# Every second quad's last 704 words of the last down unit as a transfer of its own, from an input laid out for it

## The chip, the cores and the metric

The kernel runs on one core of one Trainium2 chip. What is measured is the time on the device in microseconds (us) of one execution of the whole program; times of several runs are given as their median. The profile shows one execution.

## The reference, cut to what matters

The program is a decoder trunk of two layers for 256 tokens of width 1024 in float32. Each layer has a token mixer (heads of stick-breaking attention and retention in layer 0, sliding-window attention in layer 1) and then a mixture of experts, on which this change works:

```python
def expert_block(args):
    xb, e = args
    h = jax.nn.silu(xb @ w_gate[e]) * (xb @ w_up[e])
    return h @ w_down[e]
```

There are 32 experts in each layer, with `w_gate` and `w_up` of 1024 x 512 and `w_down` of 512 x 1024 floats: 6 MB an expert, 192 MB a layer. Each token goes to two of them. Every expert's weights are read once per layer.

## The kernel before

**Tiling.** The 32 experts of a layer are taken as 8 quads of four experts. A quad's weights are 12 units: 4 of gate, 4 of up and 4 of down. A unit is 128 partitions by `UNIT` = 4096 words (2 MB), and partition p of a unit is one contiguous run in HBM. The weights rest in SBUF in slots of one unit each. Eight of them (`LOOP_SLOTS`) form a ring for the loop over the quads.

**Loading.** SyncE (`sp`) issues all loads of weights, one queue, in a fixed order. Within `experts(l)`, quads 0 and 1 are loaded unit by unit. After that a loop runs `half` times (here 3): `quad(2 * t, 1)` and `quad(2 * t + 1, 0)`. A quad of the first sort is loaded by three transfers of 8 MB (line 590). One of the second sort, quads 3, 5 and 7, is loaded by one of 8 MB for gate (line 590), two of 4 MB for up (line 586), one of 4 MB for down units 0 and 1 (line 580), and then by `last_units` (lines 566 to 572): unit 2 whole, and unit 3 in two halves of 2048 words, 1 MB each. Each transfer counts 16 on a semaphore, one for each of 16 shares in which the DMA engines do it. Before each group of transfers SyncE waits on `m["used"]`, which TensorE raises when it has read the slots that are to be overwritten.

**Computing.** TensorE waits in `four` (lines 1398 to 1439) for the landing of a unit and multiplies the quad's tokens with it; for down, `four` is called twice and needs all four units from the first matmul, and so `low_landed` too. The quad that ends a layer (`final=True`, always of the second sort, quad 7) goes through `last_down` (lines 1465 to 1483) instead: one expert e at a time, each as its unit lands. For e = 3 it waits for `low_landed` (the low half of unit 3), does q = 0 and 1, then waits for `landed[k]` (the high half), and does q = 2 and 3. A q is 1024 words of the unit:

```python
for q in range(MH):
    if e == QUAD - 1 and q == MH // 2:
        pe.wait_ge(m["landed"][k], 16 * loads)
```

`last_combine` (line 1489 and on) then adds the expert's rows to the tokens. In layer 0 the loads of the next mixer (`w_c`) stand in the queue right behind quad 7; in layer 1 nothing does, and after the last `last_combine` come only the final norm and the output.

**Semaphores.** `x_in[0..2]` count the three pieces of the input x at the program's start and are not used later.

Of the kernel before, what the change touches and what calls it, by code (L numbers as in the profile page):

```python
# [13 lines left out]
P = 128  # L14
# [6 lines left out]
DEPTH = 2  # L21
# [31 lines left out]
UNIT = 4096  # L53
SPARE = 4
HALF_UNIT = UNIT // 2
EARLY_LOADS = 1
EARLY_UPS = ({6: (0, 1)}, {4: (0, 2), 6: (1, 3)})
SECOND_QUAD = (1, 4)
# [43 lines left out]
def chunks_aside(w):  # L102

    return np.ascontiguousarray(w.reshape(DEPTH, QUADS, QUAD, P, KD, DE).transpose(0, 1, 3, 4, 2, 5))

def column_units(w, cols):
# [49 lines left out]
    return gains.astype(f32), early.astype(f32), late.astype(f32), decay.reshape(P, -1).astype(f32)  # L157

def hybrid_trunk(nc, b_in_c, sinks, w_gate, w_up, w_down, xT, w_ab, w_c, wo_ab, wo_c, gain_table, early_table,  # L160
                 late_table, decay_table, rope_table, out):
    ctx = ExitStack()
    with ctx:
# [157 lines left out]

        gains_in, early_in, late_in = sem("gains_in"), sem("early_in"), sem("late_in")
        x_in = [sem(f"x_in{j}") for j in range(3)]
        first_in = [sem(f"first_unit_in{j}") for j in range(2)]
        decay_in, rope_in = sem("decay_in"), sem("rope_in")
        rows_in = sem("bias_rows_in")
# [187 lines left out]
        def _(sp):  # L515
# [26 lines left out]
            def experts(l):  # L542

                m = moe[l]
                last_rows = units(l, 0, QUAD_UNITS - 1)
                sp.wait_ge(once["logits"], l + 1)
                sp.wait_ge(h_put, KD * (l + 1))
                sp.dma_start(flat(hT[:]), last_rows[:, 0:HALF_UNIT]).then_inc(m["low_landed"], 16)
                sp.wait_ge(m["low_used"], 1)
                sp.dma_start(home(LOOP_SLOTS[l][0])[:, 0:HALF_UNIT], last_rows[:, HALF_UNIT:UNIT]).then_inc(m["landed"][0], 16)  # L550
                sp.wait_ge(m["low_used"], 2)
                k = ring_place((0, 0), 0)[0]
                sp.dma_start(home(LOOP_SLOTS[l][0])[:, HALF_UNIT:UNIT], units(l, 1, 0)[:, 0:HALF_UNIT]).then_inc(early_up[1], 16)
                sp.wait_ge(m["low_used"], 3)
                sp.dma_start(home(LOOP_SLOTS[l][k])[:, 0:HALF_UNIT], units(l, 1, 0)[:, HALF_UNIT:UNIT]).then_inc(m["landed"][k], 16)
                for j in range(1, QUAD_UNITS):
                    if j == 1:
                        sp.wait_ge(m["low_used"], 4)
                    elif j in (2, 3, 5, 7, 8, 10):
                        sp.wait_ge(m["used"], {2: 2, 3: 3, 5: 4, 7: 6, 8: 6, 10: 7}[j])  # L560
                    load(l, 1, j, ring_place((0, 0), j)[0])
                sp.wait_ge(once["rounds"], l + 1)
                last = sp.value_load(rounds[0:1, l, 1:2], min_val=QUADS - 1, max_val=QUADS * PASSES - 1)
                half = sp.value_load(rounds[0:1, l, 3:4], min_val=QUADS // 2 - 1, max_val=QUADS * PASSES // 2 - 1)

                def last_units(quad, k):

                    src = units_of(l, quad, QUAD_UNITS - 2, 2)
                    sp.dma_start(home(LOOP_SLOTS[l][k]), src[:, 0:UNIT]).then_inc(m["landed"][k], 16)
                    for lo, landed in ((0, m["low_landed"]), (HALF_UNIT, m["landed"][k + 1])):  # L570
                        sp.dma_start(home(LOOP_SLOTS[l][k + 1])[:, lo:lo + HALF_UNIT],
                                     src[:, UNIT + lo:UNIT + lo + HALF_UNIT]).then_inc(landed, 16)

                def quad(i, which):
                    sp.compute_val((i % QUADS) * (QUAD * D * DE) * 4)
                    for kind in range(3):
                        k = ring_place((which, 0), kind * QUAD)[0]
                        if which == 0 and kind == 2:
                            sp.wait_ge(m["used"], PER_QUAD * i + 1)
                            sp.dma_start(homes(LOOP_SLOTS[l][k], 2), units_of(l, i % QUADS, 2 * QUAD, 2)).then_inc(m["landed"][k], 16)  # L580
                            sp.wait_ge(m["used"], PER_QUAD * i + 2)
                            last_units(i % QUADS, k + 2)
                        elif which == 0 and kind == 1:
                            sp.wait_ge(m["used"], PER_QUAD * i)
                            for lead in (0, 2):
                                sp.dma_start(homes(LOOP_SLOTS[l][(k + lead) % LOOP], 2),
                                             units_of(l, i % QUADS, QUAD + lead, 2)).then_inc(m["landed"][(k + lead) % LOOP], 16)
                        else:
                            sp.wait_ge(m["used"], PER_QUAD * i + (-1, 0, 2)[kind])
                            sp.dma_start(homes(LOOP_SLOTS[l][k], QUAD), units_of(l, i % QUADS, kind * QUAD, QUAD)).then_inc(m["landed"][k], 16)  # L590

                with sp.Fori(1, half + 1) as t:
                    quad(2 * t, 1)
                    quad(2 * t + 1, 0)
                return last
# [443 lines left out]
        def _(pe):  # L1039
# [305 lines left out]
            def experts(l):  # L1345
# [51 lines left out]
                def four(place, kind, dst, lhsT, steps, cols, part=None):  # L1397

                    def slot(j):
                        return LOOP_SLOTS[l][ring_place(place, j)[0]]  # L1400

                    unit = {}
                    for s in range(QUAD if kind == 2 else 0):
                        j = QUAD * kind + s
                        if place == 0 and j - 2 * QUAD < PARKED:
                            pe.wait_ge(parked[j - 2 * QUAD], 16 * (l + 1))
                            unit[s] = slot_out(PARK_SLOTS[j - 2 * QUAD])
                        else:
                            k, loads = landing(place, j)
                            pe.wait_ge(m["landed"][k], 16 * loads)  # L1410
                            unit[s] = slot_out(slot(j))
                    if place == 0 and kind == 2:
                        pe.wait_ge(m["low_landed"], 16 * EARLY_LOADS)
                    if place != 0 and place[0] == 0 and kind == 2:
                        pe.wait_ge(m["low_landed"], 16 * (place[1] + EARLY_LOADS))
                    for q in range(*(part or (steps,))):
                        c = QUAD * kind + q // 2
                        if kind < 2 and q % 2 == 0 and (singly(place) or q == 0 or q == 4 and kind == 1 and place[0] == 0):
                            k, loads = landing(place, c)
                            pe.wait_ge(m["landed"][k], 16 * loads)  # L1420
                            if place != 0 and singly(place) and c == 0:
                                which, loads = SECOND_QUAD
                                pe.wait_ge(early_up[which], 16 * (loads if l else 1))
                            if place == 0 and c in EARLY_UPS[l]:
                                which, loads = EARLY_UPS[l][c]
                                pe.wait_ge(early_up[which], 16 * loads)
                        for s in range(QUAD):
                            rows = slice(s * CAP, (s + 1) * CAP)
                            if kind < 2:
                                half = home(slot(c))[:, q % 2 * HALF_UNIT:(q % 2 + 1) * HALF_UNIT]  # L1430
                                if place != 0 and singly(place) and c == 0:
                                    half = (home(LOOP_SLOTS[l][0])[:, HALF_UNIT:UNIT], home(slot(0))[:, 0:HALF_UNIT])[q]
                                moving = half[:, s * DE:(s + 1) * DE]
                            elif place == 0 and s == QUAD - 1:
                                moving = (*early_rows, unit[s][:, 0, :], unit[s][:, 1, :])[q][:, cols]
                            else:
                                moving = unit[s][:, q, cols]
                            op = pe.matmul(dst[rows, :], lhsT[:, q, rows], moving,  # L1438
                                           start=(q == 0), stop=(q == steps - 1))
                    return op  # L1440
# [23 lines left out]
                def last_down(e, t):  # L1464
# [9 lines left out]
                    for q in range(MH):  # L1474
                        if e == QUAD - 1 and q == MH // 2:
                            pe.wait_ge(m["landed"][k], 16 * loads)
                        by_strip = unit[:, q, :].rearrange("p (j s n) -> p s j n", j=2, s=QUAD)
                        for s in range(QUAD):
                            op = pe.matmul(bank[LAST_BANKS[e]][s * CAP:(s + 1) * CAP, 0:S], e_hT[:, q, e * CAP:(e + 1) * CAP],
# [776 lines left out]
```

## Time and profile before

| what | value |
|---|---|
| median of 3 runs | 1118.91 us |
| lowest and highest run | 1117.99 and 1121.75 us |
| span of the profiled execution | 1120.8 us |
| instructions | 13766 |
| TensorE clock, mean granted | 0.867 |
| TensorE (PE) busy | 827.4 us, 74% |
| HBM read | 436.60 MB, 390 GB/s over the span |

The profiled execution's own time is its span, 1120.8 us from the first to the last instruction; what lies around it isn't told apart, and it stands between the lowest and the highest of the three runs, 1.9 us above their median. Busy shares are means over stages with different limits, so each stage is read for itself: which wait ends last there. PE is TensorE's matmul, PEld its weight load, SPq the queue of SyncE. A DMA share of 1.00 means that all 16 DMA engines moved data through the whole stretch.

### The profile page before, as it was taken

How to read it: one execution, taken by the hardware profiler on the slowest of the kernel's cores; microseconds unless marked ns; L12 is line 12 of the kernel's file. 1: busy time of each engine (PE TensorE's matmuls, PEld its weight loads, DVE VectorE, ACT ScalarE, POOL GpSimd, SP SyncE). 2: the span in 40 equal slices, each digit the busy share in tenths (PEclk: the TensorE clock that was granted, in tenths of full speed). 3: DMA queues.
4: the chain of work that ended last, by engine and by line, in shares of the span. 5: the costliest groups of instructions: out<-in, count | busy, mean ns of one | idle time of the engine just before them, and what ended most of it. 6: DMA issues, size and time to landing. Idle time of an engine off the chain costs nothing.

```text
span 1120.8 us, 13766 instructions
## 1 busy us (share of the span) xinstructions
PE 827.4 (74%) x5882; PEld 460.5 (41%) x5882; DVE 195.7 (17%) x498; ACT 157.8 (14%) x365; POOL 58.7 (5%) x81
## 2 busy tenths in 40 slices
PE   9999999746575566648789999956556565746876
PEld 8888774312222131314447776331313122311533
DVE  2546441000000000000018635100000000000002
ACT  2225233000000000000011545100000000000102
POOL 1010020000000000000000442000000000000000
PEclk9999999968787797869989999977888777877989
DMA  9952779999999999999999659999999999999994
GB/s 377 429 210 95 308 308 424 426 443 440 417 427 443 431 431 429 441 433 428 423 418 421 249 205 372 422 436 438 436 420 430 440 436 417 427 439 440 428 425 185
DMA packets 22640, 438.37 MB, mean 391 GB/s; under 512 B 2624, under 2 KB 3648, under 8 KB 6336
## 3 DMA queue, kind: packets, MB, share of 16 engines
q1 hardware_dynamic: 21328, 434.39, 91.5%
q10 hardware_dynamic: 1264, 3.27, 0.7%
q8 instruction: 39, 0.64, 0.2%
q14 instruction: 9, 0.07, 0.0%
HBM read 436.60 MB, written 1.05 MB: 390 GB/s over the span
## 4 chain that ended last, share of the span: by engine, by line
DMA 53%; PE 43%; DVE 1%; issue 1%; ACT 1%; SPq 0%; POOL 0%; DVEq 0%; ACTq 0%; POOLq 0%
DMA store<-in_w_down 21%; DMA store<-in_w_gate 18%; PE bank L1438 18%; DMA store<-in_w_up 13%; PE bank L1110 5%; PE bank L1101 5%; PE bank L1270 5%; PE bank L1581 1%; PE bank L1041 1%; PE bank L1070 1%; PE bank L1374 1%; PE bank L1362 1%; PE bank L1461 1%; PE bank L1204 0%; PE bank L1182 0%
## 5 line engine op out<-in xcount | busy, mean ns | idle before, releaser
L1438 PE MATMUL bank<-store,hg 128*32 128x512 f32 x2048 | 279.9, 704 | 208.9 <-DMA store<-in_w_up 109.8
L1438 PEld LDWEIGHTS bank<-store,hg 128*32 128x32 f32 x2048 | 72.3, 127 | 399.1 <-issue 258.7
L1438 PE MATMUL bank<-store 128*32 128x512 f32 x880 | 120.8, 702 | 63.9 <-DMA store<-in_w_down 62.5
L1438 PEld LDWEIGHTS bank<-store 128*32 128x32 f32 x880 | 34.2, 126 | 142.8 <-issue 141.1
L2028 DVE TENSOR_TENSOR store<-store,bank 128x512 f32<-128x512 f32 x14 | 9.6, 687 | 465.7 <-PE bank L1438 465.7
L1270 PE MATMUL bank<-store 128*128 128x256 f32 x256 | 64.8, 389 | 0.5 <-ACT store L995 0.5
L1101 PE MATMUL bank<-hg,store 128*128 128x256 f32 x256 | 57.1, 383 | 0.3 <-DMA store<-w_ab 0.3
L1362 PEld LDWEIGHTS bank<-store,hr 128*128 128x128 f32 x448 | 51.5, 193 | 13.1 <-issue 13.1
L1362 PE MATMUL bank<-store,hr 128*128 128x128 f32 x448 | 54.2, 280 | 0.0
L2035 DVE COPY hg<-bank 128x512 f32<-128x512 f32 x14 | 9.7, 692 | 248.6 <-PE bank L1438 248.6
L1461 PE MATMUL bank<-store,hg 128*128 128x256 f32 x224 | 50.8, 380 | 1.4 <-ACT store L902 1.4
L1101 PEld LDWEIGHTS bank<-hg,store 128*128 128x128 f32 x256 | 48.8, 192 | 7.3 <-DMA store<-w_ab 0.6
L1270 PEld LDWEIGHTS bank<-store 128*128 128x128 f32 x256 | 45.3, 190 | 8.4 <-ACT store L995 2.5
L718 POOL TENSOR_TENSOR store<-store,gate_all 128x256 f32<-128x256 f32 x16 | 9.8, 615 | 733.7 <-PE bank L1041 702.3
L912 ACT ACTIVATE hg<-bank 128x512 f32<-128x512 f32 x14 | 8.4, 597 | 258.4 <-PE bank L1362 258.4
L1461 PEld LDWEIGHTS bank<-store,hg 128*128 128x128 f32 x224 | 41.7, 191 | 6.8 <-DVE hg L2035 1.8
L890 ACT ACTIVATE store<-bank 128x512 f32<-128x512 f32 x14 | 8.4, 597 | 222.4 <-PE bank L1438 222.4
L898 ACT ACTIVATE hg<-bank 128x512 f32<-128x512 f32 x14 | 8.4, 597 | 218.1 <-PE bank L1438 218.1
L1041 PE MATMUL bank<-early,store 128*128 128x128 f32 x180 | 30.1, 284 | 1.6 <-DVE store L2028 1.6
L1110 PE MATMUL bank<-store 128*128 128x256 f32 x136 | 31.1, 382 | 0.0
L1041 PEld LDWEIGHTS bank<-early,store 128*128 128x128 f32 x180 | 22.3, 164 | 18.3 <-issue 12.1
L1110 PE MATMUL bank<-store,hg 128*128 128x256 f32 x120 | 27.9, 381 | 0.0
(248 smaller groups left out, 688.2 us busy)
## 6 DMA issues: line engine op xcount, KB each, us to landing
store<-in_w_up SPq DMA_DIRECT2D x12, 4096.0 KB, 24.7
store<-in_w_down SPq DMA_DIRECT2D x20, 2048.0 KB, 24.2
store<-in_w_gate SPq DMA_DIRECT2D x14, 2048.0 KB, 12.5
store<-in_w_up SPq DMA_DIRECT2D x13, 2048.0 KB, 17.1
store<-in_w_down SPq DMA_DIRECT2D x6, 4096.0 KB, 23.8
store<-in_w_down SPq DMA_DIRECT2D x14, 1024.0 KB, 27.7
store<-w_ab SPq DMA_DIRECT2D x6, 2048.0 KB, 30.6
store<-in_w_up SPq DMA_DIRECT2D x5, 1024.0 KB, 5.5
```

Source lines behind the costliest of these rows:

```text
L718: pool.tensor_tensor(quad_rows(pick_w), quad_rows(pick), of_quad(gate_all, i % QUADS), ALU.mult).then_inc(m["pick_w"], 1)
L1041: return pe.transpose(dst, src, ident)
L1070: pe.matmul(bank[7][:, 0:rhs.shape[1]], lhsT, rhs, start=True, stop=True)
L1101: op = pe.matmul(dst[c // 2][:, (c % 2) * S:(c % 2 + 1) * S], slot_in(s)[:, k, c * P:(c + 1) * P], hg[:, k, :], start=(k == 0 and c % 2 == ...
L1110: op = pe.matmul(dst, x[:, k, :], w[:, k, :], start=(start and k == 0), stop=(k == 3), skip_group_check=True)
L1270: op = pe.matmul(chunk_of(H_BANKS, k), unit(c, k), t[:, 4 * part + c, :], start=(part == 0 and c == 0 and k < 4), stop=(part == 1 and c == 3),
L1362: op = pe.matmul(of_block(bank[4 + high], k), hr[:, b, 4 * high + k, :], pick[:, b, :], start=(b == 0), stop=(b == NB - 1))
L1374: op = pe.matmul(of_block(bank[at], place), hr[:, b, k, :], pick[:, b, :], start=(b == 0), stop=(b == NB - 1))
L1438: op = pe.matmul(dst[rows, :], lhsT[:, q, rows], moving, start=(q == 0), stop=(q == steps - 1))
L1461: pe.matmul(chunk_of(H_BANKS, k), e_y[:, k, :], pick_wT, start=False, stop=False, skip_group_check=True)
L1581: op = pe.matmul(bank[C_IN_BANKS[0][b]][:], hg[:, k, b * P:(b + 1) * P], slot_in(c_slot(0))[:, i, :], start=(i == 0), stop=(i == KD - 1))
L2035: dve.tensor_copy(flat(e_y[:, 0:4, :]), bank[4][:]).then_inc(m["y_low"], 1)
```

## The change

The host lays out a second copy of a part of the down weights, `down_ends`: for each layer and quad, the last 704 words (`EIGHTHS`) of each partition of the quad's unit 3, 2816 bytes a partition. It is stored as [16, 8, 704], where partition p = 16 a + b stands at [b, a]. In `last_units` the high half of unit 3 (2048 words) is cut: 1344 words come as before and count on `landed[k + 1]`; the last 704 words are a third transfer, read from `down_ends` as [8, 16, 704], which counts on a semaphore of its own for each layer (`eighths_in[l]`, the former `x_in[0]` and `x_in[1]` used again, which stand at 16 when it begins). The slowest dimension of its source has 8 entries, where that of every other transfer of weights has 128. TensorE waits for it before the down matmuls of quads 3 and 5, and in quad 7 before q = 3 of expert 3. No matmul and no byte in SBUF changes. It concerns three quads a layer, six transfers in all.

```diff
+EIGHTHS = 704
+def ends_by_eighths(w):
+    ends = w[..., -EIGHTHS:].reshape(DEPTH, QUADS, 8, P // 8, EIGHTHS)
+    return np.ascontiguousarray(ends.swapaxes(2, 3))
-        x_in = [sem(f"x_in{j}") for j in range(3)]
+        eighths_in = [sem(f"x_part{l}_then_eighths_of_layer{l}_in") for l in range(DEPTH)]
+        x_in = [*eighths_in, sem("x_in2")]
@@ last_units
-                    for lo, landed in ((0, m["low_landed"]), (HALF_UNIT, m["landed"][k + 1])):
-                        sp.dma_start(home(LOOP_SLOTS[l][k + 1])[:, lo:lo + HALF_UNIT],
-                                     src[:, UNIT + lo:UNIT + lo + HALF_UNIT]).then_inc(landed, 16)
+                    for lo, hi, landed in ((0, HALF_UNIT, m["low_landed"]), (HALF_UNIT, UNIT - EIGHTHS, m["landed"][k + 1])):
+                        sp.dma_start(home(LOOP_SLOTS[l][k + 1])[:, lo:hi], src[:, UNIT + lo:UNIT + hi]).then_inc(landed, 16)
+
+                    sp.dma_start(home(LOOP_SLOTS[l][k + 1])[:, UNIT - EIGHTHS:UNIT],
+                                 down_ends[l, bass.ds(quad, 1)].rearrange("q b a n -> (q a) b n")).then_inc(eighths_in[l], 16)
@@ four
                         pe.wait_ge(m["low_landed"], 16 * (place[1] + EARLY_LOADS))
+                        if not singly(place):
+                            pe.wait_ge(eighths_in[l], 16 * (place[1] + 1))
@@ last_down
                             pe.wait_ge(m["landed"][k], 16 * loads)
+                        if e == QUAD - 1 and q == MH - 1:
+                            pe.wait_ge(eighths_in[l], 16 * (t + 1))
@@ kernel
+    arrays["down_ends"] = ends_by_eighths(arrays["in_w_down"])
```

## Rows read from the trace of the kernel before

**Rows 1.** The page: HBM traffic and the DMA queues (packets, MB, share of 16 engines).
```profile
q1 hardware_dynamic: 21328, 434.39, 91.5%
q10 hardware_dynamic: 1264, 3.27, 0.7%
q8 instruction: 39, 0.64, 0.2%
HBM read 436.60 MB, written 1.05 MB: 390 GB/s over the span
```

**Rows 2.** The page: the chain that ended last, shares of the span by engine.
```profile
DMA 53%; PE 43%; DVE 1%; issue 1%; ACT 1%; SPq 0%; POOL 0%; DVEq 0%; ACTq 0%; POOLq 0%
```

**Rows 3.** Chain in order of time, 400 to 500 us: start, us, what.
```profile
405.11 7.11 PE bank L1438 x64
...
412.76 30.80 DMA store<-in_w_up
...
443.61 5.66 PE bank L1438 x32
...
449.28 33.26 DMA store<-in_w_gate
```

**Rows 4.** Stretches: us, busy by engine (count), PE clock, DMA share, GB/s.
```profile
212.50:572.50 360.00, 225.83 (x1674) 100.19 (x1678) 15.22 (x24) 17.39 (x34) 3.69 (x6) 0.81 1.00 431
...
740.50:1100.50 360.00, 227.47 (x1678) 101.24 (x1682) 15.10 (x24) 17.95 (x35) 3.69 (x6) 0.80 1.00 431
```

**Rows 5.** SyncE's queue in order of time, quad 5's loads of down.
```profile
429.33 0.33 SPq L580 DMA_DIRECT2D store<-in_w_down  x1
432.76 0.33 SPq L569 DMA_DIRECT2D store<-in_w_down  x1
433.31 0.96 SPq L571 DMA_DIRECT2D store<-in_w_down  x2
449.28 0.33 SPq L590 DMA_DIRECT2D store<-in_w_gate  x1
```

**Rows 6.** Line 571: durations in ns, and DMA to landing.
```profile
L571 SPq DMA_DIRECT2D store<-in_w_down x12: 332/333/337, 316.8 to 1076.8; - x12
...
DMA to landing us min/median/max: 25.9/28.2/30.5
```

**Rows 7.** Chain at the end of layer 1: start, us, what.
```profile
1076.83 30.51 DMA store<-in_w_down
1107.35 0.04 issue
1107.39 1.07 PE bank L1479 x16
1108.46 1.98 PE bank L1499 x32
```

**Rows 8.** Chain at the end of layer 0's experts.
```profile
550.82 30.05 DMA store<-in_w_down
580.87 0.04 issue
580.91 1.94 PE bank L1479 x16
582.85 2.65 PE bank L1499 x32
```

**Rows 9.** Stretches of 1 us at the end of layer 1 (columns as rows 4).
```profile
1100.00:1101.00 1.00, 1.00 (x24) 0.46 (x16) 0.00 (x0) 1.00 (x1) 0.00 (x0) 1.00 1.00 418
1101.00:1102.00 1.00, 1.00 (x20) 0.72 (x16) 0.00 (x0) 0.70 (x3) 0.00 (x0) 1.00 0.69 287
1102.00:1103.00 1.00, 0.83 (x20) 0.38 (x16) 0.00 (x0) 0.00 (x0) 0.00 (x0) 1.00 0.60 238
1103.00:1104.00 1.00, 1.00 (x27) 0.56 (x20) 0.00 (x0) 0.00 (x0) 0.00 (x0) 1.00 0.34 139
1104.00:1105.00 1.00, 1.00 (x20) 0.67 (x16) 0.00 (x0) 0.38 (x1) 0.00 (x0) 1.00 0.16 66
1105.00:1106.00 1.00, 1.00 (x24) 0.47 (x20) 0.00 (x0) 0.00 (x0) 0.00 (x0) 1.00 0.14 57
1106.00:1107.00 1.00, 0.46 (x12) 0.00 (x0) 0.00 (x0) 0.00 (x0) 0.00 (x0) 1.00 0.08 33
```

**Rows 10.** Stretches of 1 us where the queue next runs dry after layer 0.
```profile
622.00:623.00 1.00, 1.00 (x6) 0.84 (x5) 0.81 (x5) 0.02 (x1) 0.00 (x0) 1.00 0.88 352
623.00:624.00 1.00, 1.00 (x6) 0.60 (x4) 0.96 (x6) 1.00 (x5) 0.00 (x0) 1.00 0.61 233
624.00:625.00 1.00, 1.00 (x10) 0.66 (x10) 0.23 (x1) 1.00 (x6) 0.00 (x0) 1.00 0.39 156
625.00:626.00 1.00, 1.00 (x5) 0.90 (x6) 0.92 (x5) 0.30 (x1) 0.48 (x1) 1.00 0.23 90
626.00:627.00 1.00, 1.00 (x6) 0.87 (x6) 0.97 (x8) 0.84 (x4) 1.00 (x2) 1.00 0.05 20
```

**Rows 11.** DMA queues in the stretch from 1080 to 1090 us.
```profile
q1 hardware_dynamic: 144, 4.19, 97.8%
q8 instruction: 1, 0.02, 0.7%
```

More of the change, by code:

```diff
@@ L157, in tables, with hybrid_trunk @@
     return gains.astype(f32), early.astype(f32), late.astype(f32), decay.reshape(P, -1).astype(f32)
-def hybrid_trunk(nc, b_in_c, sinks, w_gate, w_up, w_down, xT, w_ab, w_c, wo_ab, wo_c, gain_table, early_table,
+def hybrid_trunk(nc, b_in_c, sinks, w_gate, w_up, w_down, down_ends, xT, w_ab, w_c, wo_ab, wo_c, gain_table, early_table,
                  late_table, decay_table, rope_table, out):
```

## The prediction

> **What bounds the kernel now.** I read the page first. The chain that ended last is DMA for 53% and TensorE for 43% [rows 2], and HBM is read at 390 GB/s over the whole span [rows 1], so transfers bind in part of the program. Then the stages: in 360 us of each layer's experts the DMA share is 1.00 and the rate 431 GB/s [rows 4]. All 16 engines are at work all the time, at 431 / 16 = 26.9 GB/s each. The two stretches hold 720 of 1120.8 us. The chain in order of time shows what that looks like from TensorE [rows 3]: 31 to 33 us on a transfer, then 6 to 7 us of matmuls. These matmuls are on that chain only because SyncE issues the next load after them; a load waits its turn for 28.2 us from issue to landing [rows 6], though 1 MB at 431 GB/s takes 2.4 us. So some 25 us of work lie queued ahead, no engine runs dry, and a matmul made faster there gives nothing.
>
> What matters then is how long each engine needs for its own share of the bytes. A transfer has landed when its last share has. I looked for a spread where nothing is queued behind: the end of layer 1. There the DMA share falls over 6 us, not at once: 1.00, 0.69, 0.60, 0.34, 0.16, 0.14, 0.08 [rows 9]. Times 16, that is 16, 11.0, 9.6, 5.4, 2.6, 2.2 and 1.3 engines at work. So the eighth engine is done near 1103.1 us, fourteen near 1104.6, and **two engines work alone** for the last 2 us, until TensorE's wait ends at 1107.35 [rows 7]. The missing shares from 1101 us on sum to 0.31 + 0.40 + 0.66 + 0.84 + 0.86 + 0.92 = 4.0 us: with even loads the landing could come about 4 us earlier. After layer 0, where the queue next runs dry, the fall has the same form (0.88, 0.61, 0.39, 0.23, 0.05) and takes some 5 us [rows 10]. One source shows: instructions are fetched by the same engines, 16 KB at a time; the one fetch between 1080 and 1090 us holds 0.7% of 160 engine-us, 1.1 us of one engine [rows 11]. Thirty-nine of them fall on single engines [rows 1], and an engine that never runs dry never catches up.
>
> **The change, part by part.** Its core: 704 words of 128 partitions, 360 KB, go in eight shares, not sixteen.
>
> With sixteen shares an engine moves 22.5 KB of it, 22.5 / 26.9 = 0.84 us. With eight, eight engines move 45 KB and eight nothing. No row shows a transfer of eight shares. The bytes cost 1.68 us at 26.9 GB/s. For short packets the nearest row is queue 10: 0.7% of 16 x 1120.8 us for 1264 packets of 2.6 KB on average, 0.10 us each, 26 GB/s [rows 1], which makes 16 packets of 2816 bytes 1.7 to 1.75 us. So per transfer the eight loaded engines lose 0.9 us and the eight spared ones win 0.84. Three such transfers stand between a layer's start and its end: **2.7 us later on eight engines, 2.5 us earlier on the other eight**.
>
> What that gives depends on which eight are spared; no view names an engine. Say first that the two stragglers are among them. Layer 1: they come at 1107.35 - 2.5 = 1104.85. The loaded engines are at best the first eight to finish, 1103.1 + 2.7 = 1105.8: gain 1.5 us. If one of the loaded stands among the next six (up to 1104.6), it ends at 1107.3: gain 0. That all eight loaded ones are the first eight is unlikely, that one is the very last of the six too; I take the middle, 0.7 us. Layer 0: the end of quad 7 is covered by the next loads, so its spread is read from the fall after it, where the last engines trail by less (0.23 and 0.05 in the last two us, where layer 1 has 0.16, 0.14 and 0.08): I take 0.4 us, between 0 and 1.2.
>
> The second gain is sure: in quad 7 TensorE waits for the 704 words only before q = 3. The wait before q = 2 now needs only 1344 words, which land earlier by at least the last share's 0.84 us, so q = 2 of expert 3 comes off the end. Sixteen matmuls (q = 2 and 3) take 1.94 us in layer 0 and 1.07 in layer 1 [rows 7, 8]; half, 0.97 and 0.53. In layer 0 the 0.84 limits it. **Sum: 0.84 + 0.53 = 1.4 us.**
>
> Small costs. SyncE: one more issue, 0.33 us [rows 6], six times, with 0.1 us of address work. It lies after the two of line 571, and the next load is issued 15 us later, as it must wait for TensorE [rows 5]: hidden, and behind it only that load is queued, which needs 25 us until its landing. If the cover were gone it would be 6 x 0.45 = 2.7 us. TensorE: ten more waits on semaphores. A wait that is met shows as 0.02 to 0.05 us on the chain [rows 7, 8]; those of quads 3 and 5 lie where TensorE waits for down units anyway, those of quad 7 on the end: 0.1 us. The matmuls of the quad are queued behind them. TensorE reads no other data; HBM gives the same bytes.
>
> Sum of the likeliest case: 0.7 + 0.4 + 1.4 - 0.1 = 2.4 us less. The profile's 1120.8 becomes 1118.4. The runs' median is 1.9 us under the span, and it is against the median that the forecast is given: 1118.9 - 2.4 = **1116.5 us**. The case spans 1.2 us less (only q = 2) to 4.0 us less (1.5 + 1.2 + 1.4 - 0.1).
>
> **Rivals.**
>
> (A) *The stragglers are loaded, not spared.* Then the end of each layer comes 2.7 us later on them, and q = 2 gives back 1.4: 2 x 2.7 - 1.4 + 0.1 = 4.1 us more, 1123.0 us. It decides from the point where one late engine of the two is among the eight that carry 45 KB. For it: no view says which engines are late, and a fetch may hit any. Against it: the two late ones trail by so much that the delay looks like one that strikes the same engines again.
>
> (B) *Eight shares get in each other's way.* The sixteen ordinary shares never slow each other (431 GB/s, share 1.00) [rows 4], but a transfer in blocks of 16 neighbouring partitions writes to SBUF in another pattern than those. If two shares that meet take turns, it runs at half speed, 3.4 us for 1.7, and the eight engines lose 2.5 us per transfer, 7.5 in a layer; the first eight then end at 1103.1 + 7.5 = 1110.6, 3.3 us after the end of now. With 3 us in layer 0 too and q = 2 given back, 4.9 us more, 1123.8 us. If instead the spared engines are only held up by what they were spared, the time falls by q = 2 alone, 1117.6. I put the middle at 1120.
>
> The trace can't show this. The Trainium skill, SBUF — State Buffer, section Door 1: The DMA port swizzle, states that four neighbouring partitions share a port and that partitions p and p + 32 are on the same one. 
>
> (C) *It doesn't do what it says*: the transfer is still done in sixteen shares. Then only q = 2 comes off: 1.3 us less, 1117.6 us.
>
> No row bears on the number of shares. The Trainium skill, DMA: Bandwidth & Descriptors, section Why a DMA increments its semaphore by 16 and not by 1, states that the number of engines is the largest up to 16 that divides the slowest dimensions of both sides, and that the lowest-numbered are used: here 8, always the same ones. By that rule C falls away.
>
> **How the numbers follow.** Likeliest case 0.52, A 0.25, B 0.13, C 0.10. Runs of one kernel scatter by 3.8 us, so a median can tell about 0.3% (3.4 us) from no change. Faster by more than that (under 1115.5): the far part of the likeliest case, 0.2. Slower (over 1122.3): most of A and a third of B, 0.24. Within: 0.56. Range: from 1114.8, just beyond the likeliest case's best of 1114.9, to 1123.2, which takes in A; the rest of B and a scatter of the medians stay out. The likeliest case alone: 1114.9 to 1117.7.
>
> **What would show it.** At the end of layer 1, the fall of the DMA share: if eight engines carry more, some eight stay at work together (share near 0.5) and the two-engine tail (0.14, 0.08) is gone; with A the tail is longer, with C as now. In the chain, TensorE's last L1479 piece is 8 matmuls, not 16. The new issue stands behind line 571's with 0.33 us, and 128 packets more of under 4 KB per transfer appear in the queue. B shows as a rate under 431 GB/s around the transfers of quads 3 and 5. Wrong would be: queues that run dry, or a change of the end of layer 0 that the next mixer swallows.

## The result, and the profile after

The changed kernel takes **1140.2 us** (median of 5 runs, 1135.8 to 1143.0), beside 1119.7 us for the kernel before (5 runs, 1118.0 to 1121.8): ratio 1.0169, 95% interval 1.0154 to 1.0185. It is slower by 1.7%, some 20 us, and the time lies far above the range. The profiled execution took 1137.6 us with a span of 1135.7, so it stands 14.9 us over the span of before; the ledger below is made between these two. The other 5.6 us of the difference of the medians are not in it: the profiled execution of after is 2.5 us under its median, and that of before is a long one of its kernel. In every later run with both numbers the time is 1.8 to 2.0 us more than the span, so by estimate that execution took some 1122.7 us, 3.0 over its median.

The page of after: span, packets, queue 1 and HBM.

```profile
span 1135.7 us, 13792 instructions
...
DMA packets 23456, 438.37 MB, mean 386 GB/s; under 512 B 2672, under 2 KB 3696, under 8 KB 7920
...
q1 hardware_dynamic: 22144, 434.39, 91.5%
...
HBM read 436.60 MB, written 1.05 MB: 385 GB/s over the span
```

The same bytes as in [rows 1], and the same 91.5% of busy engines over a span that is 1.3% longer: the engines work longer for the same bytes. The two 360 us stretches of the experts say it directly (columns as in [rows 4]):

```profile
212.50:572.50 360.00, 218.37 (x1598) 95.88 (x1597) 14.10 (x23) 17.01 (x33) 3.70 (x6) 0.81 1.00 426
740.50:1100.50 360.00, 220.27 (x1612) 96.67 (x1612) 14.56 (x23) 16.42 (x32) 3.70 (x6) 0.81 1.00 426
```

The share is still 1.00, but the rate is 426 GB/s, not 431 [rows 4]: 1.2% of 360 us, 4.2 us in each. No queue ran dry.

**Where it is lost.** The chain of waits is the ruler here. From the piece of matmuls that follows the landing of an up load to the piece that follows the landing of the next gate load lies always the same queue of bytes, and in the kernel before this takes the same time at each place. After, layer 0 and layer 1 (start, us, what):

```profile
325.07 6.05 PE bank L1450 x32
...
366.67 9.16 PE bank L1450 x64
...
444.10 6.27 PE bank L1450 x32
...
486.56 8.94 PE bank L1450 x64
...
859.70 4.99 PE bank L1450 x32
...
900.37 8.55 PE bank L1450 x64
...
1058.92 7.11 PE bank L1450 x64
```

And the kernel before, the places that [rows 3] doesn't hold:

```profile
326.59 6.14 PE bank L1438 x32
...
365.66 8.80 PE bank L1438 x64
...
482.68 10.02 PE bank L1438 x64
...
853.25 5.64 PE bank L1438 x32
...
892.32 10.00 PE bank L1438 x64
```

Differences of starts. Quad 3 of layer 0: 365.66 - 326.59 = 39.07 us before, 366.67 - 325.07 = 41.60 after, **+2.5**. Quad 5: 39.07 before (482.68 - 443.61), 42.46 after, **+3.4**. Quad 3 of layer 1: 39.07 and 40.67, **+1.6**. Quad 5 of layer 1, read the same way, 39.06 and 40.62, +1.6. In each case one transfer of 704 words lies within the stretch, and the bytes are the same. The two in quad 7 are read from the landing of the load of down before it to the last landing: in layer 1, 1119.98 - 1058.92 = 61.06 against 59.61 before, **+1.5**; in layer 0, +2.4. The six make 12.9 us. Between these stretches -1.5, -0.5 and +1.6 us, with smaller ones, cancel but for 0.3. Two kernels below in which nothing is lost (e1, e5) show the ruler's own scatter: their stretches of quads 3 and 5 take 39.1 to 39.2 us, those of quad 7 58.1 to 59.6. So the four differences of quads 3 and 5, 9.1 us, are clear of it, and of each of the two in quad 7 some 1.5 us can be scatter. The last landing is 12.6 us late:

```profile
1086.84 33.14 DMA store<-down_ends
1119.98 0.04 issue
1120.02 1.08 PE bank L1493 x8
1121.11 3.77 PE bank L1513 x32
```

The wait ends at 1119.98, not at 1107.35 [rows 7]. The remaining 2 us are behind it. Eight matmuls now take 1.08 us, as long as sixteen did, and the 32 after them 3.77 us instead of 1.98 [rows 7]. The 1 us stretches of after's end show why, and how the queue runs dry:

```profile
1110.00:1111.00 1.00, 1.00 (x20) 0.50 (x16) 0.00 (x0) 0.99 (x3) 0.00 (x0) 1.00 0.84 352
1111.00:1112.00 1.00, 0.88 (x16) 0.45 (x12) 0.00 (x0) 0.31 (x2) 0.00 (x0) 1.00 0.79 326
1112.00:1113.00 1.00, 0.95 (x20) 0.61 (x24) 0.00 (x0) 0.00 (x0) 0.00 (x0) 1.00 0.78 314
1113.00:1114.00 1.00, 1.00 (x24) 0.42 (x16) 0.00 (x0) 0.00 (x0) 0.00 (x0) 1.00 0.61 232
1114.00:1115.00 1.00, 1.00 (x16) 0.63 (x16) 0.00 (x0) 0.38 (x1) 0.00 (x0) 1.00 0.64 193
1115.00:1116.00 1.00, 0.06 (x4) 0.00 (x0) 0.00 (x0) 0.00 (x0) 0.00 (x0) 1.00 0.58 128
1116.00:1117.00 1.00, 0.40 (x8) 0.29 (x12) 0.00 (x0) 0.00 (x0) 0.00 (x0) 1.00 0.24 80
1117.00:1118.00 1.00, 0.67 (x16) 0.13 (x4) 0.00 (x0) 0.00 (x0) 0.00 (x0) 1.00 0.10 39
1118.00:1119.00 1.00, 0.76 (x8) 0.16 (x8) 0.00 (x0) 0.00 (x0) 0.00 (x0) 0.68 0.07 25
1119.00:1120.00 1.00, 0.27 (x4) 0.00 (x0) 0.00 (x0) 0.00 (x0) 0.00 (x0) 0.50 0.03 11
```

TensorE had little to do from 1115 on (busy 0.06, 0.40 and 0.67), and its granted clock then fell from 1.00 over 0.68 to 0.50, from 2.4 to 1.2 GHz, just when the last 40 matmuls came: 4.85 us, where the last 48 took 3.05 before, **+1.8 us**. (At a clock of 1.00 such 40 take 2.62 us in e1 and e2 below, so the clock cost 2.2 and the eight matmuls fewer gave back 0.4.) 12.6 + 1.8 = 14.4 of the 14.9 us.

The same stretches say who is late. The shares from 1110 on sum to 4.68 us, so the sixteen engines finish at 1114.7 on average; before, the shares from 1101 on sum to 2.01, 1103.0 on average [rows 9]. The average is 11.7 us later, the last one 12.6. Of both, 6.3 us are layer 0's (its last landing came at 587.17, not at 580.87 [rows 8]), which leaves for layer 1 alone +5.4 us on average and +6.3 for the last. The latest engine of before would stand at 1107.35 + 6.3 = 1113.65, so whatever still works after that has lost time in layer 1; in 1114 to 1115 and 1115 to 1116 these are ten and nine engines (0.64 and 0.58 x 16), and only eight have a share of the transfer. **So engines without a share lose too.** If no engine lost more than the last one's 6.3 us, eight alone could move the average by 3.2 at most, and it moved by 5.4: by that estimate nearly all lose. And in 1115 to 1116 the nine engines move 128 GB/s, 14 each, where an engine of the full stream moves 26.9: with little queued beside them, the eight shares run at about half speed.

SyncE's queue and the new issue (line 581; ns min/median/max):

```profile
435.58 0.71 SPq L581 DMA_DIRECT2D store<-down_ends  x1
450.39 0.34 SPq L600 DMA_DIRECT2D store<-in_w_gate  x1
...
L581 SPq DMA_DIRECT2D store<-down_ends x6: 646/687/859, 316.6 to 1086.8; - x6
```

It takes twice what one issue of line 571 takes [rows 6], and 14 us pass before SyncE is wanted again.

### The profile page after: what moved, and what is told of

Read it like the earlier page. It is cut to its first block, busy times and chain, and to the rows that moved or that the text cites. A ratio compares the mean times of both kernels' runs of the same rounds, so it can differ in the third digit from the quotient of the medians.

```text
span 1135.7 us, 13792 instructions
## 1 busy us (share of the span) xinstructions
PE 823.1 (72%) x5882; PEld 460.3 (41%) x5882; DVE 195.9 (17%) x498; ACT 158.0 (14%) x365; POOL 58.8 (5%) x81
## 3 DMA queue, kind: packets, MB, share of 16 engines
q1 hardware_dynamic: 22144, 434.39, 91.5%
## 4 chain that ended last, share of the span: by engine, by line
DMA 54%; PE 42%; DVE 1%; issue 1%; ACT 1%; SPq 0%; POOL 0%; DVEq 0%; ACTq 0%; POOLq 0%
DMA store<-in_w_gate 19%; PE bank L1450 17%; DMA store<-in_w_down 16%; DMA store<-in_w_up 13%; DMA store<-down_ends 6%; PE bank L1120 5%; PE bank L1111 5%; PE bank L1280 5%; PE bank L1595 1%; PE bank L1051 1%; PE bank L1080 1%; PE bank L1384 1%; PE bank L1372 1%; PE bank L1513 1%; PE bank L1473 1%
## 5 line engine op out<-in xcount | busy, mean ns | idle before, releaser
L1450 PE MATMUL bank<-store 128*32 128x512 f32 x880 | 113.1, 664 | 70.9 <-DMA store<-in_w_down 44.2
```

The costliest lines, as they stand in the source:

```text
L1450: op = pe.matmul(dst[rows, :], lhsT[:, q, rows], moving, start=(q == 0), stop=(q == steps - 1))
```

## The experiments

Three things changed at once: the unit's end is a third transfer with its waits; it comes from a dense copy; and it goes in eight shares of 16 neighbouring partitions. The theories: **P**, the form of the shares: an engine writes partitions that other engines write in an ordinary transfer, and both suffer; **L**, the load on eight engines; **H**, the source in HBM; **W**, the cut, its issue and waits. The kernel before ran beside each group: 1120.0, 1120.6, 1119.9 and 1120.5 us. "Ordinary" is the form of all other loads, [128 partitions, n] from rows in order.

**e1: the cut, but sixteen ordinary shares.**

```
-   down_ends[l, bass.ds(quad, 1)].rearrange("q b a n -> (q a) b n"))
+   src[:, 2 * UNIT - EIGHTHS:2 * UNIT])
```

> The changed kernel, but the last 704 words come from the old input with 128 rows as the slowest dimension, so in sixteen shares. The cut into three transfers, the extra issue and the waits are all kept. Theory P (shares in blocks of neighbouring partitions meet at the way into SBUF and slow all engines): all of the loss is gone, and what the later wait before q = 3 gives stays: 1118 to 1119 us against 1119.7 before. Theory W (the third transfer, its issue or its waits cost): 1135 us or more, as changed. Theory S (eight engines carry too much) and theory H (the new copy is read badly from HBM): as P.

Measured: 1120.2 us, ratio 0.9997 (0.9987 to 1.0008). Its end:

```profile
1076.43 30.22 DMA store<-in_w_down
...
1106.69 0.64 PE bank L1493 x8
1107.33 1.98 PE bank L1513 x32
```

Three transfers instead of two, six issues more, ten waits more: nothing. W falls. The last wait is now followed by 8 matmuls of 0.64 us, not by 16 of 1.07, so 0.43 us of the gain from moving q = 2 are there in the trace; the median doesn't show them and stays above the 1118 to 1119 us expected, and the interval lets the gain be 1.5 us at most.

**e2: sixteen shares of 8 neighbouring partitions.** All engines carry the same.

```
-   ends = w[..., -EIGHTHS:].reshape(DEPTH, QUADS, 8, P // 8, EIGHTHS)
+   ends = w[..., -EIGHTHS:].reshape(DEPTH, QUADS, 16, P // 16, EIGHTHS)
```

> The changed kernel, but the copy is laid out so that the slowest dimension of the source has 16 entries: sixteen shares of 8 neighbouring partitions each. All engines carry the same bytes again, but each share is a block of neighbours, and the copy is read with rows of different shares between each other, as in the change. Theory P: a good part of the loss stays, 1126 to 1140 us. Theory S: no loss, 1118 to 1119 us. Theory H: the loss stays, 1135 to 1140.

Measured: 1136.6 us, ratio 1.0143 (1.0125 to 1.0161). The ruler at quad 5 of layer 0, and the end:

```profile
445.94 5.07 PE bank L1450 x32
...
487.90 2.74 PE bank L1450 x9
...
1120.05 0.64 PE bank L1493 x8
1120.69 1.98 PE bank L1513 x32
```

487.90 - 445.94 = 41.96 us, +2.9. With even loads its last landing is as late as that of eight shares (1120.05 and 1120.02). So most of the loss comes without L (16.6 of 20.5 us by the medians). Of the 2.7 us by which its span (1133.0) is shorter than the change's, 2.2 are in the last 40 matmuls: 2.62 us, as the granted clock here stayed at 1.00 to the end.

**e3: the copy holds each share's rows side by side.** Eight shares as in the change; a row left free behind every 16 keeps the shares apart.

```
-   return np.ascontiguousarray(ends.swapaxes(2, 3))
+   apart = np.zeros((DEPTH, QUADS, 8, P // 8 + 1, EIGHTHS), ends.dtype)
+   apart[:, :, :, :P // 8] = ends
+   return apart
...
-   down_ends[l, bass.ds(quad, 1)].rearrange("q b a n -> (q a) b n"))
+   down_ends[l, bass.ds(quad, 1), :, 0:P // 8].rearrange("q a b n -> (q a) b n"))
```

> The changed kernel, but the copy holds each share's 16 rows one behind the other, with a row left free between shares (so that the source still has 8 as its slowest dimension): each of the eight engines reads one run of 45 KB. Theory H: the loss is gone, 1118 to 1124 us. Theories P and S: as changed, 1135 to 1143 us.

Measured: 1139.6 us, ratio 1.0155 (1.0126 to 1.0184): as the change. For eight shares the order of the rows in HBM doesn't matter.

**e5: the dense copy, sixteen ordinary shares.**

```
-   ends = w[..., -EIGHTHS:].reshape(DEPTH, QUADS, 8, P // 8, EIGHTHS)
-   return np.ascontiguousarray(ends.swapaxes(2, 3))
+   return np.ascontiguousarray(w[..., -EIGHTHS:])
...
-   down_ends[l, bass.ds(quad, 1)].rearrange("q b a n -> (q a) b n"))
+   down_ends[l, bass.ds(quad, 1)].rearrange("q p n -> (q p) n"))
```

> The changed kernel, but the copy is plain: 128 rows of 704 words one behind the other, read with 128 rows as the slowest dimension, so in sixteen ordinary shares. It has the small, dense source of the changed kernel with the ordinary way of sharing out. Theory P (shares of neighbouring partitions are what disturbs): as before, 1118 to 1122 us. Theory H2 (a dense source of 360 KB is slow to read for all engines at once): the loss stays, 1133 to 1140.

Measured: 1120.2 us, ratio 1.0003 (0.9990 to 1.0017). With e3, H falls. Here and in e2 the cut is the same, the copy is dense and there are sixteen shares; they stand 16 us apart, and with the order in HBM ruled out by e3, what differs is which partitions a share has.

**m1: the transfers alone.** Only SyncE's transfers: each form by itself, then each with 8 MB queued behind it.

```
+   def shares(k, each):
+       return bass.AP(rows.tensor, rows.offset, [[N, k], [k * N, each], [1, N]])
...
+   sp.dma_start(odd[:], shares(8, 16)).then_inc(lone, 16)
```

> Not the model: only transfers of one input into SBUF by SyncE, each shape on a line of its own, three times; the output is a copy of x. First each shape alone, with nothing beside it (704 words a partition: sixteen ordinary shares; 8 shares of 16 partitions; 16 shares of 8; 8 shares of 8 on partitions 0 to 63; 8 shares of 4 on partitions 0 to 31, and on 64 to 95), then each with an 8 MB transfer queued behind it. Theory P: alone, 8 shares of 16 take well over twice the time that an ordinary share's 8 rows take in excess of the fixed part, since shares 0 and 2 (partitions 0 and 32) meet, 8 shares of 8 on 64 partitions are slowed too (0 and 4 meet), and 8 shares of 4 are not, as each has its own way. With 8 MB behind, 8 shares of 4 on partitions 0 to 31 cost the 8 MB nothing (the same engines serve these partitions in an ordinary transfer) and on 64 to 95 they do. Theory S: time goes by the rows per engine alone (16 rows 1.8 us, 8 rows 0.9, 4 rows 0.45, plus some 2 us fixed), and the 8 MB land later by the rows of the fullest engine.

SyncE's queue of m1, the first four trials of the first round; a trial ends where the next issue starts:

```profile
9.40 0.34 SPq L43 DMA_DIRECT2D odd<-rows  x1
12.44 0.78 SPq L46 DMA_DIRECT2D odd<-rows  x1
17.52 0.59 SPq L49 DMA_DIRECT2D odd<-rows  x1
21.46 0.63 SPq L52 DMA_DIRECT2D odd<-rows  x1
```

Ordinary 3.0 us (12.44 - 9.40); eight shares of 16 partitions 5.1; sixteen of 8 partitions 3.9; eight of 8 partitions 3.7; eight of 4, on partitions 0 to 31 and on 64 to 95, 2.5 and 2.65. The two later rounds are within 0.25 us of these. With 8 MB behind: 22.4 to 22.9 us ordinary, 24.8 to 25.5 in eight blocks, 23.4 to 24.8 in sixteen, and 22.75 to 22.9 for eight shares of 4 at either place. A part of what P expected came: of the 0.9 to 1.1 us that sixteen blocks take more, only 0.25 is the longer issue (line 49, 0.59 us, line 43, 0.34). What P expected of the place, that 64 to 95 costs the 8 MB behind something and 0 to 31 doesn't, didn't come. The next test needed the stream ahead and behind.

**m2: a transfer in the middle of a stream.** 8 MB, the small transfer, 8 MB, all queued at once.

```
+   sp.dma_start(flow[:], weights[:]).then_inc(led, 16)
+   sp.dma_start(odd[64:96], shares(8, 4)).then_inc(lone, 16)
+   sp.dma_start(more[:], weights[:]).then_inc(followed, 16)
```

> Not the model: only transfers, three times over. Each trial is 8 MB, one small transfer (or none), 8 MB, with all three in the queue at once, and its time is from the first issue to that of the next trial. Sixteen ordinary shares of 704 words: 0.8 us over none. Eight shares of 4 partitions, 1408 words, on 0 to 31: 0.8 to 0.9 us over none; on 64 to 95: 2 to 3 us over none. Sixteen blocks of 8 partitions, 704 words: 3 us over; eight blocks of 16: 3 us or more over.

SyncE's queue of m2, first round: the trials on partitions 0 to 31, on 64 to 95 and the start of the next.

```profile
92.94 0.33 SPq L59 DMA_DIRECT2D flow<-weights  x1
...
134.82 0.33 SPq L66 DMA_DIRECT2D flow<-weights  x1
...
177.83 0.33 SPq L73 DMA_DIRECT2D flow<-weights  x1
```

From start to start: 180 KB in eight shares of 4 partitions take 134.82 - 92.94 = 41.88 us on partitions 0 to 31 and 177.83 - 134.82 = 43.01 on 64 to 95. In the same way nothing between the two 8 MB takes 41.28, 360 KB ordinary 42.19, in sixteen blocks of 8 partitions 43.03, in eight blocks of 16 44.96. The medians of the rounds, less the bare stream's 41.27: +0.9 ordinary, +0.6 and +1.5 for the two places, +1.8 and +3.6 for the blocks. So the cost is there without TensorE and without this kernel: 0.9 us for the place alone, 0.8 for sixteen blocks and 2.7 for eight against the ordinary form. But for the place and for sixteen blocks it is less than was expected (2 to 3 us and 3 us over none), and less than in the kernel, where the same two come to 1.8 (d3 less d2, below) and 2.8 us (e2) per transfer.

**d1, d2, d3, d4: the load and the partitions apart.** The kernel before stays whole and gets a transfer more after line 571's, whose words nobody uses; TensorE waits for it as in the change. d1: 704 words, 128 partitions, ordinary, so all sixteen engines carry 22.5 KB more. d2: 1408 words to partitions 0 to 31 in eight shares of 4 partitions, the same 22.5 KB more for eight engines. d3 and d4: the same to partitions 64 to 95 and 32 to 63.

```
+   # d1
+   sp.dma_start(flat(hT[:])[:, 0:EIGHTHS],
+                down_ends[l, bass.ds(quad, 1)].rearrange("q p n -> (q p) n")).then_inc(eighths_in[l], 16)
...
+   # d2; d3 has 64:96, d4 has 32:64
+   sp.dma_start(flat(hT[:])[0:32, 0:WIDE],
+                down_ends[l, bass.ds(quad, 1)].rearrange("q b a n -> q (b a n)")[:, 0:8 * 4 * WIDE]
+                .rearrange("q (b a n) -> (q a) b n", b=4, a=8)).then_inc(eighths_in[l], 16)
```

> The kernel before, with one transfer more in each of the six places: 704 words of 128 partitions into a part of SBUF that is free then, in sixteen ordinary shares. Its result is not used. It is the price of 22.5 KB more on every engine, undisturbed: 6 x 0.84 = 5.0 us, so 1124 to 1126 us by every theory.

> As d1, but the transfer goes to partitions 0 to 31 alone, 1408 words each, in eight shares of 4 partitions: the same 22.5 KB on each of eight engines, nothing on the other eight. Theory P with the places of an ordinary transfer (engine a serves partitions 4a to 4a + 3 there too): nobody is disturbed, the price is at most that of d1 and less if the last engines are not among the eight: 1120 to 1125 us. Theory S (load on eight engines is what hurts): 1124 us or more.

> As d2, but to partitions 64 to 95: the same eight engines, the same bytes, the same rows, only other partitions, which in an ordinary transfer other engines serve. Theory P: these eight shares meet the running transfers of the other engines; slower than d2 by 1 to 2 us for each of the six, 1127 to 1136 us. Theory S: equal to d2 within 1 us.

> As d2 and d3, but to partitions 32 to 63. If what counts is that an engine writes only where it also writes in an ordinary transfer, and an ordinary transfer gives each engine four partitions below 32 and the four that lie 32 higher: as d2, 1120 to 1123 us. If an ordinary transfer gives each engine eight neighbouring partitions (engine a serves 8a to 8a + 7), d2 and this would each be foreign for most engines, and this one, where no engine of the eight but the upper four has its place, would cost as d3: 1130 us or more.

Measured: d1 1124.4 us, 1.0032 (1.0019 to 1.0046), +3.8 us. d2 1121.5, 1.0008 (0.9997 to 1.0020), +0.9. **d3 1132.1, 1.0102 (1.0074 to 1.0129), +11.5.** d4 1121.8, 1.0015 (0.9999 to 1.0030), +1.2. The ruler at quad 5 of layer 0, first d2, then d3:

```profile
443.96 6.52 PE bank L1451 x32
...
483.03 6.97 PE bank L1451 x41
```

```profile
446.26 6.29 PE bank L1451 x32
...
487.04 3.59 PE bank L1451 x13
```

39.07 us in d2, as if there were no transfer more; 40.78 in d3. In the 360 us of layer 0's experts the rates lie apart as well, d2 and then d3:

```profile
212.50:572.50 360.00, 228.70 (x1665) 101.23 (x1667) 14.61 (x24) 17.32 (x34) 3.70 (x6) 0.81 1.00 431
```

```profile
212.50:572.50 360.00, 222.09 (x1621) 98.22 (x1620) 14.99 (x24) 17.02 (x33) 3.70 (x6) 0.81 1.00 427
```

Same bytes, rows, number of shares and issue; only the partitions differ, and 10.6 us hang on them. That is P. No view names an engine, so the partitions might also decide which engines carry the shares. But 22.5 KB more on all engines cost only 3.8 us (d1), so the choice of engines doesn't make d3's 11.5. The Trainium skill, SBUF — State Buffer, section Door 1: The DMA port swizzle, puts partitions p and p + 32 on one port and p + 64 on another; DMA: Bandwidth & Descriptors, section The descriptor swizzle, has each engine write one port of its own in a 128-partition transfer, the first eight engines partitions 0 to 63. The runs agree in all three places: 0 to 31 and 32 to 63 cost next to nothing, 64 to 95 ten times that. d1 against d2 says something of its own: 22.5 KB more on all engines cost 3.8 us, on these eight alone 0.9. So the engines that finish last are, it seems, mostly not among these eight.

**e4: 352 words instead of 704.**

```
-EIGHTHS = 704
+EIGHTHS = 352
```

> The changed kernel with 352 words for 704. If the loss goes with the bytes that are written from the wrong engines: half of it, 1128 to 1132 us. If each transfer costs a fixed stall: 1136 to 1140.

Measured: 1126.2 us, ratio 1.0055 (1.0034 to 1.0076): +6.3, a third of the change's 20. There is no fixed price per transfer; half the bytes cost less than half, below the 1128 us expected at least. In its trace the ruler has +0.6, +0.8 and +0.5 us in layer 0 and +1.5, +1.5 and 0 in layer 1, 4.9 us for the change's 12.9, and the last 48 matmuls ran at a granted clock of 0.50, 5.73 us for 3.05: of the 4.5 us by which the span is longer than before (1125.3), 2.7 are the clock.

**e6: four transfers of 32 partitions each, in eight shares of 4.** By the mapping above, the first two of the four then write where their engines always write.

```
-   ends = w[..., -EIGHTHS:].reshape(DEPTH, QUADS, 8, P // 8, EIGHTHS)
-   return np.ascontiguousarray(ends.swapaxes(2, 3))
+   ends = w[..., -EIGHTHS:].reshape(DEPTH, QUADS, 4, 8, 4, EIGHTHS)
+   return np.ascontiguousarray(ends.swapaxes(3, 4))
...
+   for part in range(4):
+       sp.dma_start(home(LOOP_SLOTS[l][k + 1])[32 * part:32 * part + 32, UNIT - EIGHTHS:UNIT],
+                    down_ends[l, bass.ds(quad, 1), part].rearrange("q b a n -> (q a) b n")).then_inc(eighths_in[l], 16)
```

> The changed kernel, but its transfer is made as four of 32 partitions, each in eight shares of 4 partitions. The same eight engines carry the same 45 KB, but on partitions 0 to 63 each now writes where it writes in an ordinary transfer, and only 64 to 127 are foreign. Theory P: the loss halves, to about the price of d3: 1127 to 1134 us (three more issues of 0.3 to 0.7 us each are hidden). Theory S: no difference to the change, 1137 to 1140.

Measured: 1133.1 us, ratio 1.0132 (1.0106 to 1.0158), +13.2. A third of the loss is gone, not a half. It is close to d3's 11.5, and in both 180 KB go to partitions of other engines; in the change nearly all 360 KB do. That the loss goes with these bytes is argued from three numbers, and e4 lies below such a line: not shown.

## Why the prediction was wrong

- **What binds**: right. Transfers set the time, the queue never ran dry, and what TensorE or SyncE gained or paid in e1 was nothing that its median shows. At the end of the changed kernel TensorE's clock cost 2.2 us, a term that the sum didn't have.
- **The load, +2.7 and -2.5 us a layer**: right in direction; its size alone was not seen. d2 gives eight engines 22.5 KB more per transfer, and it costs 0.9 us in all, where d1, on all engines, costs 3.8. That speaks against rival A: with a late engine among the eight, d2 would cost about what d1 does. But the gain that was to follow (0.7 + 0.4 us) could not appear, as the spared engines weren't spared. No run spares engines by shares that stay on their own partitions, so whether it exists is open.
- **Rival B was the mechanism, and it was mis-sized.** The step that failed is the sentence that eight shares at half speed cost "2.5 us per transfer" on the eight engines alone, read off only at the two layer ends, with the spared engines at worst "held up by what they were spared". It priced a transfer that is slow by itself. The half speed is there at the end of the queue (14 GB/s an engine). But what the runs show beyond it is a transfer that slows the ordinary stream around it: more engines than have a share, 1.5 to 3.4 us at each of six places, 12.9 us between them, and since no queue runs dry, none of it is made up before the layer's end. B's middle, 1120 us, came from an end of 1123.8 that was itself 16 us too low, and its chance of 0.13 kept even that out of the range. Nor were A and B put together; with B's 7.5 us a layer on a late engine they would give 2 x 7.5 - 1.4 + 0.1 = 13.7 us more, 1132.6, nearer to what came, but not by what happened: e2 loads no engine more and loses 16.6.
- **"The sixteen ordinary shares never slow each other"** was read rightly [rows 4] and used wrongly. It holds for shares that each keep to their own partitions: e2 has sixteen shares and even loads too, and loses 16.6 us.
- **"The second gain is sure", 1.4 us**: not sure. The piece of 8 matmuls is there as forecast, in after and in e1, and at the end of layer 1 e1's trace shows 0.43 us for the forecast 0.53; for layer 0's 0.84 there is no fair reading, as the kernel before ran its last matmuls there at a granted clock of 0.50 and e1 at 1.00. e1's median stands within 0.3 us of that of the kernel beside it, with up to 1.5 us of gain allowed. In after, the granted clock took more than the gain: the 8 matmuls took 1.08 us, what 16 took before.
- **SyncE, 0.33 us and hidden**: hidden, yes (e1, e5), but 0.69 us. The row was one of an ordinary source. **TensorE's waits, 0.1 us**: too small to see, as said.
- **Rival C** (still sixteen shares) falls: 1117.6 us is not what came. The page has 22144 - 21328 = 816 packets more on queue 1, 136 per transfer, with 128 forecast [rows 1].
- **What would show it** did: the rate under 431 GB/s around quads 3 and 5. The drain has the share near 0.6 in three stretches (0.61, 0.64, 0.58), nine or ten engines where eight were forecast, but then the tail of one or two engines is there as before (0.10, 0.07, 0.03), where the likeliest case had it gone.
- **The 1.9 us from the span to the median** that the forecast took off is not what lies between a span and a time: in every later run the span is the shorter, by 1.8 to 2.0 us. The profile of before is of a long execution. It did no harm, as the forecast was put against the median.

Open: why one transfer costs 1.5 us and another 3.4 (in after those of layer 0 cost more than those of layer 1, but in e2 quads 3 and 5 pay +3.1 and +2.9 in layer 0 and +2.6 and +3.0 in layer 1, so the layer isn't the reason); why transfers that meet on an idle chip (m1) and in a bare stream (m2) lose less than in the kernel; why 352 words cost less than half and four transfers more than half. That a shared port of SBUF is the place of it is an inference from which partitions cost and which don't; no view shows a port.

## What to carry to other kernels

In this kernel, whose stream is bound by transfers, it counted for more which partitions each share of a transfer goes to than how evenly bytes are spread over the engines. So shift load between engines only with shares that stay on the partitions that each engine writes anyway. Before such a change is made, run its two halves as controls: the same cut in the ordinary form (here free), and the odd form with even loads (here 16.6 us). A disturbance of a queue that never runs dry is to be priced at each transfer, on the stream around it, and not at the stage's end on the engines it was meant for.

## What the runs showed of the hardware

- An extra 180 KB in a full stream costs 0.9 us in six transfers on partitions 0 to 31, 1.2 us on 32 to 63 and 11.5 us on 64 to 95, from the same eight shares (d2, d4, d3). In a bare stream the place alone costs 0.9 us per transfer (m2).
- Partitions 0 to 31 and 64 to 95 differ on an idle chip by 0.15 us or less (m1): a price taken there would have missed it.
- The cut, a dense copy as source, six issues and ten waits are free to within 0.2% (e1, e5).
- Issuing a transfer whose shares interleave in the source takes SyncE 0.6 to 0.9 us, an ordinary one 0.33 to 0.35 (0.43 right behind another, m2).
- The last 40 matmuls after a wait took 2.6 us where the granted clock stayed at 1.00 (e2) and 4.85 where it had fallen to 0.50 (after); before it fell, TensorE's busy share had been 0.06, 0.40 and 0.67. So a late landing can cost more than its lateness, here 2.2 us.
